# Attention value products of two query tiles in one set of 256-column matmuls

## What is computed

```
for l in range(2):
    sh1, sc1, gt1, sh2, sc2, gt2 = adaln(c, w_ada[l], b_ada[l])     # and the same for c_ctx
    qa, ka, va, fb, qc, kc, vc = mixer_inputs(h, w_in[l], ...)      # 6 query heads of 64 twice, 2 kv heads
    o = concatenate([global_attention(qa, ka, va, kac, vac),        # 512 keys: context and own
                     fourier_mix(fb),
                     window_attention(qc, kc, vc, kcc, vcc, sink[l])])
    x = x + gt1 * (o @ w_out[l])
    if l == 0:                                                      # the context stream: 256 keys
        oc = concatenate([dense_attention(qac, kac, vac), fourier_mix(fbc), dense_attention(qcc, ...)])
        ctx = ctx + cgt1 * (oc @ w_out[l])
softmax(q k^T / 8) @ v, per head, 128 queries at a time
```

## Time and profile before

| | |
|---|---|
| time, median of 3 runs | 1571.26 us (1570.78 to 1572.89) |
| time of the profiled execution | 1570.74 us |
| its span, first to last instruction | 1568.7 us |
| PE busy | 1519.9 us (97%) |
| DVE busy | 993.4 us (63%) |
| ACT busy | 676.1 us (43%) |
| `att1` of layer 0, of layer 1 | 107.8 to 218.9 us, 703.1 to 769.5 us |

### The profile page before, as it was taken

One profiled execution on the slowest core, in us unless ns is written; L12 is line 12 of the kernel. 1 busy time (PEld: TensorE's weight loads), 2 busy tenths in 40 slices (PEclk: granted clock), 3 DMA queues, 4 the chain that ended last, 5 costly groups with the idle time before them and its releaser, 6 DMA issues.

```text
span 1568.7 us, 23749 instructions
## 1 busy us (share of the span) xinstructions
PE 1519.9 (97%) x9371; PEld 1256.2 (80%) x9371; DVE 993.4 (63%) x1491; ACT 676.1 (43%) x1055; POOL 133.1 (8%) x132
## 2 busy tenths in 40 slices
PE   6999999999999999999989999899999999999998
PEld 3765468988888888884689999788989978898896
DVE  2758645445434456858656667778865767877566
ACT  3445434321212212535453333565555646446463
POOL 1210001100000000410010000312000111200002
PEclk9999999999999999999999999999999999999999
DMA  9436852323232232238745555555533455463342
GB/s 335 162 105 229 285 135 83 102 85 107 81 107 85 102 105 83 87 103 314 197 135 188 179 184 182 173 167 156 184 112 119 150 169 174 135 215 108 119 143 88
DMA packets 168991, 234.22 MB, mean 149 GB/s; under 512 B 8976, under 2 KB 116536, under 8 KB 168768
## 3 DMA queue, kind: packets, MB, share of 16 engines
q1 hardware_dynamic: 168896, 232.90, 45.7%
HBM read 231.83 MB, written 1.05 MB: 148 GB/s over the span
## 4 chain that ended last, share of the span: by engine, by line
PE 85%; DVE 7%; ACT 3%; DMA 2%; POOL 2%; issue 2%; SPq 0%; POOLq 0%; DVEq 0%; ACTq 0%
PE psum L751 24%; PE psum L753 23%; PE psum L752 23%; PE psum L1025 3%; PE psum L1058 3%; PE psum L1045 3%; PE psum L766 2%; DVE wl L1777 2%; DMA raw<-in_w_ada 1%; PE psum L953 1%; DVE smax L2100 1%; PE psum L885 1%; ACT wh L1330 1%; PE psum L1097 1%; ACT hTh L1552 1%
## 5 line engine op out<-in xcount | busy, mean ns | idle before, releaser
L1777 DVE TENSOR_TENSOR wl<-raw,wh 128x2048 fp32r<-128x2048 f32 (+1 forms) x170 | 384.9, 2264 | 245.0 <-ACT wh L1667 149.6
L751 PE MATMUL psum<-hTh,wh 128*128 128x256 f32 (+1 forms) x1376 | 428.3, 311 | 4.6 <-DVE hTl L1900 3.1
L752 PE MATMUL psum<-hTl,wh 128*128 128x256 f32 (+1 forms) x1376 | 423.1, 307 | 0.0
L753 PE MATMUL psum<-hTh,wl 128*128 128x256 f32 (+1 forms) x1376 | 423.0, 307 | 0.0
L751 PEld LDWEIGHTS psum<-hTh,wh 128*128 128x128 f32 x1376 | 262.2, 191 | 22.8 <-issue 5.7
L1667 ACT ACTIVATE wh<-raw 128x2048 fp32r<-128x2048 f32 x62 | 118.9, 1917 | 364.5 <-PE psum L753 364.5
L752 PEld LDWEIGHTS psum<-hTl,wh 128*128 128x128 f32 x1376 | 262.4, 191 | 12.9
L753 PEld LDWEIGHTS psum<-hTh,wl 128*128 128x128 f32 x1376 | 262.3, 191 | 12.5
L1330 ACT ACTIVATE wh<-raw 128x2048 fp32r<-128x2048 f32 (+2 forms) x108 | 202.5, 1875 | 109.3 <-PE psum L753 98.3
L751 PE MATMUL psum<-wh,hTh 128*128 128x512 f32 (+3 forms) x576 | 221.9, 385 | 8.9 <-DVE hTl L1879 4.1
L753 PE MATMUL psum<-wh,hTl 128*128 128x512 f32 (+3 forms) x576 | 218.2, 379 | 0.0
(11 more groups left out here) (193 smaller groups left out, 1717.5 us busy)
## 6 DMA issues: line engine op xcount, KB each, us to landing
raw<-in_w_in SPq DMA_DIRECT2D x54, 1024.0 KB, 5.0
raw<-in_w_ada SPq DMA_DIRECT2D x48, 1024.0 KB, 6.1
raw<-in_w_gate SPq DMA_DIRECT2D x22, 1024.0 KB, 5.1
raw<-in_w_up SPq DMA_DIRECT2D x22, 1024.0 KB, 5.1
raw<-in_w_down SPq DMA_DIRECT2D x22, 1024.0 KB, 4.8
raw<-in_w_in SPq DMA_DIRECT2D x16, 768.0 KB, 4.3
raw<-in_w_out SPq DMA_DIRECT2D x8, 1024.0 KB, 4.9
raw<-in_w_out SPq DMA_DIRECT2D x16, 384.0 KB, 6.6
```

What stands on the lines that cost most here:

```text
L751: pe.matmul(o, left[0], right[0], start=first, stop=False)
L752: pe.matmul(o, left[0], right[1], start=False, stop=False)
L753: return pe.matmul(o, left[1], right[0], start=False, stop=last)
L1777: dve.tensor_tensor(wl[:, w % SPLIT, 0:m], raw[:, u % RING, 0:m], wh[:, w % SPLIT, 0:m].bitcast(F32), ALU.subtract).then_inc(lo_ready, 1)
```

## The change

In the first block `values` does nothing for the first step of a pair. In the second step it makes both tiles' products: each matmul streams 256 columns, 128 from either `probT` buffer. `pv_done` is raised twice there, by the last matmul of each head. `keep_turned` of a pair's first step now waits for one count more, since the pair before reads both buffers only then.

```
 def values(u):
+    if not second and u["n"] == 0:
+        return
     pe.wait_ge(probT_ready, u["turn1"])
     at = OUT
+    if not second:
+        bank(at)
+        n = u["w"] // P
+        both = work[:, 3072:5120].rearrange("p (t c q) -> p t c q", t=2, q=P)
+        for c_ in range(n):
+            for x in range(2):
+                mm = pe.matmul(ps[at][HD * x:HD * x + HD, 0:SEQ].rearrange("p (t q) -> p t q", t=2),
+                               u["vs"][x][c_], both[:, :, n * x + c_, :], start=c_ == 0,
+                               stop=c_ == n - 1, skip_group_check=True)
+                if (c_, x) == (n - 1, 0):
+                    mm.then_inc(pv_done, 1)
+        mm.then_inc(pv_done, 1)
+        freed[at] = (mix_split, u["pair"] + 1)
+        return
...
 def keep_turned(j):
     u = steps[j]
     if j >= 2:
-        act.wait_ge(pv_done, u["step"] - 1)
+        act.wait_ge(pv_done, u["step"] - 1 + (not second and u["n"] == 0))
```

## The result

The changed kernel takes 1585.05 us (median of 4 runs, 1581.84 to 1586.16) against 1571.02 us for the kernel before (4 runs on the same chip). The ratio is 1.0085, 95% interval 1.0066 to 1.0104: slower by 10 to 16 us. Forecast were 1580.0 and 1574 to 1586. The profiled execution took 1581.84 us, the fastest of the four, with a span of 1579.9: 11.2 us more than before in the trace, where the forecast had 9.4.

What follows compares the result with a forecast made beforehand. PE was taken as the bound (97% of the span). From 1570.74 us, less 2.0 for products, plus 11.4 of net new waits, came 1580.1 us, slower by 0.6%; range 1574 to 1586, value 1580.

Steps and rivals of the forecast that it cites:

- the mechanism: `att1`: later wait on ACT delays `lead`, then `keep_mixed` and side work on DVE, so PE waits; chance 0.81.
- costed at nothing: `att1`: turning banks, logits' banks, `OUT` and each stage's last pair were priced at no new PE wait.
- Products: PE in `att1`: 0.17 us saved per pair, 18 pairs, 3.1 us; 1.89 us for a pair's group of 512 keys.
- first slot: Start of layer 0's products: PE waits for DVE anyway, 1.03 us longer, so saving falls from 3.1 to about 2 us.
- The chain: Layer 0, iteration 12: DVE gets `lead` at T plus 3.04, L766 starts at plus 4.71, PE waits 2.6 us.
- the turning bank: PE's turns in `att1`: ACT's copies end early enough, so no wait was priced.
- The other waits: Layer 0 iterations 14, 20, 22: 0.9, 1.2, 2.2 us; 9 and 11: 1.1; layer 1 iterations 10, 6, 8: 2.3, 1.7, 1.5.
- weight loads: Layer 0, around iterations 9 and 11: 0.7 us more PE wait where a load is asked for sooner than it can land.
- the last pair of each stage: End of each `att1` stage: `lead` comes later but `wout1` needs it only in its second half; no cost.
- the later wait on ACT: `keep_turned` of even steps waits for step j-1's products, delaying what is queued behind; new PE waits of 14.2 us, 11.4 net.
- the seven places: Waits priced one by one: layer 0 iterations 12, 14, 20, 22 (2.6, 0.9, 1.2, 2.2 us); layer 1 6, 8, 10 (1.7, 1.5, 2.3).

Runs made afterwards that it cites:

- e6: e4 with the first pair of layer 0 and each stage's last pair making products per tile in its own step, no side piece moved there: 1571.64 us.
- e2: Changed kernel with two more `probT` buffers, so no copy waits for the pair just before: 1574.59 us.
- e3: Changed kernel, two buffers, with `lead` put ahead of the turn's copies on ACT: 1576.70 us.
- e4: e2 with the first side piece moved between logits and turn in iterations without products: 1575.83 us.
- e5: Changed kernel with both tiles' products made in two sets of 128 columns, 32 records in place of 16: 1584.44 us.
- e7: e3 with the side pieces moved as in e4, two buffers only: 1575.89 us.
- e8: e6 with side pieces moved ahead of the turn only in iterations that still have logits: 1571.79 us.

## Why the prediction was right

The sign, the mechanism and the range held; what was off is what it costed at nothing, one attribution and the size.

- **Products.** 18 pairs at 0.17 us: PE's busy time fell by 3.0 us (3.1 forecast). A group takes 1.87 us (1.89). The first slot's idle time rose from 0.18 us to 1.25, so 1.07 us were lost there (1.0).
- **The chain.** From the products' end, DVE got `lead` at plus 2.97 us (forecast 3.04), PE started L766 at plus 4.67 (4.71). PE was there at plus 2.39, not 2.09, since its turn came 0.26 us later than worked out; 0.18 of that is a wait for the turning bank, which was costed at nothing. So the wait was 2.28 us instead of 2.6.
- **The other waits**, measured and in brackets forecast: layer 0, iteration 14 0.88 (0.9), 20 0.91 (1.2), 22 2.22 (2.2), 9 and 11 together 0.81 and 0.27 (1.1); layer 1, iteration 10 2.29 (2.3), 6 1.65 (1.7), 8 1.49 (1.5). For weight loads PE waits 1.6 us, 0.4 more than before (0.7). Together 13.2 us, against 14.2.
- **Off: costed at nothing.** "Costed at nothing: ... the last pair of each stage, whose `lead` comes later". What counts there is not `lead` but the products: PE waits 1.45 us in layer 1 for the copies of the last turn. Before, the first tile's products covered 1.03 us of that and 0.43 was left, which the prediction took off as contained in its other waits; in e6, with that pair apart, 0.43 is what it is again. This is most of what layer 1 has over the forecast 3 us (4.4). In layer 0 three smaller waits were costed at nothing: 0.5 us for ACT's copies of the Fourier products, 0.2 more in front of L1113, and the 0.18 above.
- **Off: what the waits are due to.** The prediction put them under the later wait on ACT. The products missing between the pieces were in its working (PE reaches the second piece sooner), but not named as a cause with a price of its own. At the seven places PE waits 1.0 us before the change, 11.7 in the changed kernel and still 6.1 both in e2, where ACT doesn't hold anything, and in e3, where it still does but lets `lead` go first. So about half of the new waits come from `lead` standing behind the wait, and the other half, 5.1 us, from the missing cover, of which e4 takes 3.7 us away at these places. With the first slot and the last pair that outweighs the 3.0 us that are saved, and so e2 too is slower than before.
- **Size.** The trace has plus 11.2 us, the medians plus 14.0. PE's idle time in the two stages rose by 13.6 us, where 12.4 was forecast (11.4 net and 1.0 in the first slot). That it comes so close is in part luck: the waits that were priced came out 1.0 us smaller together, and those costed at nothing added 1.9. Two of the three runs without a trace show a mean granted clock of 0.994 instead of 0.996, and in e4 the three slowest of twelve runs (1580 to 1581 us) are those with 0.993, against 0.995 to 0.997 in the others. e5's trace shows that a wait as the change has it can cost 1.6 us more, with the clock at 0.50 behind it, and the clock also fell behind waits in e4, e7 and e8. So some of the new waits may cost more in the runs that have no trace; for those runs it isn't shown.

That no variant beats the kernel before is seen in three places where the saving goes: into the weight load of layer 0 (e6, e8), into waits of side work that nothing covers any longer (e2, e8), and into the group starts that have to come back at the ends (e6).

## What to carry to other kernels

Before two pieces of work are merged to save their fixed cost, look at what the piece that is moved away was covering: on an engine that is busy 97% of the time, the small product between two links of a chain was worth 1 us as cover and 0.17 us as a group start. If a wait has to come later, look at every instruction queued behind it on that engine, and put the ones whose operands are ready ahead of it: here that one exchange gave back 8 of 14 us. And when the merged work holds a buffer for longer, price a second buffer before the wait.

## What the runs showed of the hardware

- The granted clock fell behind some waits and not behind others of the same length: behind 2.69 us in e4 its mean was 0.59 over the next 3.2 us, behind 2.22 us in e8 0.63 over 2.4 us. Behind the same 2.28 us wait in front of the same group it was 0.50 in e5, where the group took 3.54 us, and 1.00 in the changed kernel, where it took the usual 1.92. So neither the length of the wait nor its place decides it alone; what does was not tried.
- The end of a weight load was slow: in e8 PE waited from 192.06 to 194.28 while the DMA engines were busy 6% and moved 22 GB/s. The kernel before has the same, and in e8 the end of the wait has no traffic at all (windows with columns as above, the kernel before and then e8):

```profile
193.56:194.79 1.23, 0.00 (x1) 0.00 (x1) 0.00 (x0) 0.77 (x5) 0.00 (x0) 1.00 0.06 23
```

```profile
194.00:194.25 0.25, 0.00 (x0) 0.00 (x0) 0.00 (x0) 0.00 (x0) 0.00 (x0) 1.00 0.00 0
```

In the kernel before the bulk had been moved by then, at 401 to 412 GB/s (186 to 190 us). What PE waited for is the last bytes, by the single packets in e8's trace: from 192.14 to 193.97 us packets of 2 KB follow one another, one every 80 ns, each 84 ns long, where three such rows ran side by side at 191.8. One such row alone is what one of the 16 DMA engines would show (a sixteenth is 0.06; the records don't name the engine): the others were done, and it had 1.8 us of its share left. PE started 0.3 us behind the last packet.
